# Two-block model kernel: rotary tiles taken from the projection's PSUM bank, swaps placed inside the projections, values projected last

## What is computed (reference, cut)

```python
def apply_rope(x, cos, sin):                      # first block, heads of 64
    xs = x.reshape(x.shape[:-1] + (2, 2, HEAD_DIM // 4))
    rot = jnp.stack([-xs[..., 1, :], xs[..., 0, :]], axis=-2).reshape(x.shape)
    return x * cos[None, :, None, :] + rot * sin[None, :, None, :]

for layer in range(2):                            # first block
    h_x, h_c = modulate(rmsnorm(x, ...), ...), modulate(rmsnorm(ctx, ...), ...)
    mixer = mixer_ab if layer == 0 else mixer_c   # differential + neighbourhood; grouped, banded, sinks
    x = x + gate * mixer(h_x, h_c)
    x = x + gate * swiglu(modulate(rmsnorm(x, ...), ...), w1, w3, w2)
    ...                                           # the same for ctx in layer 0

# mixer_c: q 1024, k 256, v 256 columns of h @ w_in; apply_rope on q_x and k_x, not on the context's
# swa_sink_attention (a0, a3): q 1024, k 256, v 256 columns of x @ w_qkv
    q = apply_rope_2(q, cos, sin); k = apply_rope_2(k, cos, sin)
    scores = where(valid, q @ k.T * HD ** -0.5, NEG)
    probs = softmax(concat([scores, sink]))[..., :-1]
    return (probs @ v) @ w_o
# mla_attention (m2): c = x @ w_down; cq, ckv, k_rope = split(c, [384, 640])
    q_nope, q_rope = split(rms_norm(cq) @ w_uq); k_nope, v = split(rms_norm(ckv) @ w_ukv)
    q_rope, k_rope = apply_rope_2(q_rope), apply_rope_2(k_rope)

for l in range(4):                                # second block
    x = layer_norm(ALPHA * x + mixer_l(x))
    x = layer_norm(ALPHA * x + memory_cross_attention(x))
    x = layer_norm(ALPHA * x + conv_glu_ffn(x))
```

## Time and profile before

| what | value |
|---|---|
| median of 3 runs | 2978.76 us (2978.33 to 2980.78) |
| the profiled execution's own time | 2978.18 us |
| its span in the trace | 2976.2 us |
| TensorE busy | 2682.5 us, 90% |
| TensorE weight loads (overlap) | 2507.1 us, 84% |
| POOL busy | 1872.4 us, 63% |
| ScalarE busy | 1472.4 us, 49% |
| VectorE busy | 1110.4 us, 37% |
| mean granted clock of TensorE | 0.951 |
| read from HBM | 418.52 MB, 141 GB/s over the span |

### The profile page before, as it was taken

The page is one execution under the profiler, slowest core; times in us unless marked ns, Lnnn a source line. Parts: engine busy times, 40 slices in busy tenths (PEclk is TensorE's granted clock), DMA queues, the critical chain, the costliest instruction groups (busy, mean ns, idle before and its releaser), DMA issues.

```text
span 2976.2 us, 54012 instructions
## 1 busy us (share of the span) xinstructions
PE 2682.5 (90%) x19652; PEld 2507.1 (84%) x19652; DVE 1110.4 (37%) x2614; ACT 1472.4 (49%) x2572; POOL 1872.4 (63%) x789
## 2 busy tenths in 40 slices
PE   5999898999988989998889987899888899888997
PEld 2887778999976789997889987799868899777997
DVE  3126634111144521225343365433343433463334
ACT  4316644434444544445555565555545555454555
POOL 6436646878845778872468855388635588525686
PEclk8998999999999999999999998999999999989999
DMA  6224434545533545541345533255323355313453
GB/s 242 88 75 144 147 113 132 186 162 177 184 112 128 184 148 179 186 148 66 109 135 184 182 121 115 91 178 182 134 85 114 110 181 184 133 58 114 143 182 127
DMA packets 115043, 421.45 MB, mean 142 GB/s; under 512 B 12768, under 2 KB 13792, under 8 KB 114400
## 3 DMA queue, kind: packets, MB, share of 16 engines
q1 hardware_dynamic: 114336, 413.39, 41.9%
q10 hardware_dynamic: 576, 6.23, 0.5%
HBM read 418.52 MB, written 1.05 MB: 141 GB/s over the span
## 4 chain that ended last, share of the span: by engine, by line
issue 46%; POOL 28%; PE 23%; DVE 2%; ACT 1%; POOLq 1%; ACTq 0%; DVEq 0%
POOL ring_low L1972 28%; PE bank L545 7%; PE bank L546 7%; PE bank L547 7%; ACT ring_high L1036 0%; POOLq L1975 0%; DVE rstd L1461 0%; DVE scr L1440 0%; PE bank L661 0%; PE bank L658 0%; POOLq L1971 0%; DVE scr L1516 0%; ACT xt L1113 0%; ACT high L1115 0%; DVE xt L1539 0%
## 5 line engine op out<-in xcount | busy, mean ns | idle before, releaser
L1972 POOL TENSOR_TENSOR ring_low<-ring,ring_high 128x1024 fp32r<-128x1024 f32 x785 | 1872.2, 2406 | 1082.7 <-ACT ring_high L1036 734.8
L545 PE MATMUL bank<-high,ring_high 128*128 128x256 f32 (+1 forms) x4052 | 1200.6, 296 | 156.9 <-DVE low L1523 59.9
L546 PE MATMUL bank<-low,ring_high 128*128 128x256 f32 (+1 forms) x4052 | 1191.4, 294 | 0.0
L547 PE MATMUL bank<-high,ring_low 128*128 128x256 f32 (+1 forms) x4052 | 1190.4, 294 | 0.0
L545 PEld LDWEIGHTS bank<-high,ring_high 128*128 128x128 f32 x4052 | 800.4, 198 | 180.5 <-DVE low L1523 63.4
L546 PEld LDWEIGHTS bank<-low,ring_high 128*128 128x128 f32 x4052 | 800.2, 197 | 8.6
L547 PEld LDWEIGHTS bank<-high,ring_low 128*128 128x128 f32 x4052 | 799.4, 197 | 8.7
L1237 ACT ACTIVATE ring_high<-ring 128x1024 fp32r<-128x1024 f32 x462 | 479.0, 1051 | 33.4 <-PE bank L545 33.3
L1036 ACT ACTIVATE ring_high<-ring 128x1024 fp32r<-128x1024 f32 x323 | 338.6, 1053 | 181.5 <-PE bank L545 87.3
L545 PE MATMUL bank<-hid_high,ring_high 128*128 128x256 f32 x1232 | 350.2, 284 | 9.7 <-DVE hid_low L1732 9.7
L546 PE MATMUL bank<-hid_low,ring_high 128*128 128x256 f32 x1232 | 349.5, 284 | 0.0
(11 more groups left out here) (195 smaller groups left out, 2842.7 us busy)
## 6 DMA issues: line engine op xcount, KB each, us to landing
ring<-in_units SPq DMA_DIRECT2D x785, 512.0 KB, 3.3
xt<-in_x ACTq DMA_DIRECT2D x1, 2048.0 KB, 14.0
nbias<-in_bias ACTq DMA_DIRECT2D x1, 1536.0 KB, 7.8
consts<-in_consts ACTq DMA_DIRECT2D x1, 1472.0 KB, 8.3
vt<-in_mem ACTq DMA_DIRECT2D x1, 1024.0 KB, 7.4
out_x<-xt SPq DMA_DIRECT2D x8, 128.0 KB, 1.7
cols<-in_cols SPq DMA_DIRECT2D x1, 711.0 KB, 8.1
```

Of the source, the lines that this page charges most:

```text
L545: first = pe.matmul(out, w[0], x[0], start=start, stop=False, **more)
L546: pe.matmul(out, w[0], x[1], start=False, stop=False, **more)
L547: return first, pe.matmul(out, w[1], x[0], start=False, stop=stop, **more)
L1972: pool.tensor_tensor(whole(ring_low, u), whole(ring, u), whole(ring_high, u).bitcast(fp32), ALU.subtract).then_inc(unit_ready, 1)
```

## The change

Four things, all by hand in the engines' programs. (1) **Formula.** VectorE no longer reads an evacuated tile. `spin` waits for the projection's bank and makes two products of it: bank x (-scale) x sin into a scratch slot (`turned`), bank x scale x cos into the tile itself. TensorE swaps the scratch slot instead of the tile, and `rope` is one addition of bank 4 or 5 and the tile. ScalarE evacuates none of these tiles; in `ab` and for the keys of `c` it still copies the context's half (`context_half`), and the spin there waits for it. (2) **Place of the swaps.** The swap of tile m is issued behind tile m + 1 of the same projection (the keys' two behind the first query tile; in `ab` behind tile m + 3; in `m2` behind the next query tile, the last behind the first key tile, and that of the down projection's tile 5 behind the first norm's statistics). (3) **Order.** In `c`, `a0` and `a3` the projection order, and the order of the weight units, is keys, queries, values instead of keys, values, queries; the last query tile's swap stands behind the values. (4) **Feeds.** Where ScalarE no longer evacuates it runs the feeds alone (`feed_each`); in `a0` and `a3` one more `feed`, `late=UNITS[st] + 11`, stands in the second item of the attention, and in `c` two feeds of the twelve now stand with the values. `release` is also called on the matmuls of the attention's probabilities x values, all but the last of an item.

In `ab` VectorE does four spins, then four additions, twice, ahead of the values' copies. In `m2` the squares of the first norm are no longer queued on ScalarE behind the evacuation of tile 5, and the spin of that tile stands ahead of the first norm on VectorE, its addition behind the second norm.

```diff
+        def turned(slot):
+            return scr[:, 4096 + T * (slot % 4):4096 + T * (slot % 4) + T]
...
-                def rotate(st, m, src):
+                def rotate(st, m, slot=0):
                     b = 4 + m % 2
                     claim(b)
                     pe.wait_ge(*when(st, "out", m))
-                    pe.matmul(banks[b][:, 0:T], const("swap", P), src, start=True, stop=True
+                    pe.matmul(banks[b][:, 0:T], const("swap", P), turned(slot + m), start=True, stop=True
                               ).then_inc(*mark(rot_ready, st, "rot", m))
-                    reader[b] = (st, "rotread", m)
+                    reader[b] = (st, "rope", m)
...
+                                if at < len(blocks) - 1:
+                                    release(mm)
...
-                project("ab", UNITS["ab"], 16, split(0, 2 * T), 2 * T, ready=lambda k: ("n01", "h", k))
+                def turn_ab(m):
+                    if m - 3 in ROT0:
+                        rotate("ab", m - 3)
+
+                project("ab", UNITS["ab"], 16, split(0, 2 * T), 2 * T, ready=lambda k: ("n01", "h", k), after=turn_ab)
                 project_v("ab", UNITS["ab"] + 16, 4, tokens(0, 2 * T), 4)
-                for m in ROT0:
-                    rotate("ab", m, (Q2 if m < 8 else K2)(m % 8)[:, 0:T])
...
+                def turn_behind(q, k):
+                    def after(m):
+                        if m == 0:
+                            rotate(k, 0, 2)
+                            rotate(k, 1, 2)
+                        else:
+                            rotate(q, m - 1)
+                    return after
...
                         project(st + "k", u, 2, split(0), T, ready=xready)
-                        for m in range(2):
-                            rotate(st + "k", m, K1(m))
-                        project_v(st + "v", u + 2, 1, tokens(0), 2)
-                        project(st + "q", u + 4, 8, split(0), T)
-                        for m in range(8):
-                            rotate(st + "q", m, Q1(m))
+                        project(st + "q", u + 2, 8, split(0), T, after=turn_behind(st + "q", st + "k"))
+                        project_v(st + "v", u + 10, 1, tokens(0), 2)
+                        rotate(st + "q", 7)
...
-                        rotate(st + "d", 5, K1(8))
                         stats(st + "cq", None, tiles=3)
+                        rotate(st + "d", 5)
                         stats(st + "ckv", None, tiles=2)
                         project(st + "uq", UNITS[st + "_uq"], 12, split(0), T, depth=3, per_unit=2,
-                                ready=lambda k: (st + "cq", "h", k))
-                        for m in range(4):
-                            rotate(st + "uq", 8 + m, Q1(8 + m))
+                                ready=lambda k: (st + "cq", "h", k),
+                                after=lambda m: rotate(st + "uq", m - 1) if m > 8 else None)
                         up = lambda k: split(0)(4 + k)
                         project(st + "uk", UNITS[st + "_ukv"], 8, up, T, depth=2, per_unit=4,
-                                ready=lambda k: (st + "ckv", "h", k))
+                                ready=lambda k: (st + "ckv", "h", k),
+                                after=lambda m: rotate(st + "uq", 11) if m == 0 else None)
...
+                def context_half(st, tiles, dst, u0, scale=1.0):
+                    for m in tiles:
+                        feed(u0 + m)
+                        act.wait_ge(*when(st, "proj", m))
+                        act.activation(dst(m)[:, T:2 * T], banks[m % 4][:, T:2 * T], ACT.Copy, scale=scale
+                                       ).then_inc(*mark(act_done, st, "half", m))
+
+                def feed_each(u0, n):
+                    for m in range(n):
+                        feed(u0 + m)
...
+                        if s == 1 and late is not None:
+                            feed(late)
...
-                        evacuate(st + "k", 2, K1, UNITS[st])
-                        evacuate(st + "q", 8, Q1, UNITS[st] + 4, scale=lambda m: -HD ** -0.5)
-                        attention(st + "t", gqa_items(256, swa_masks, True, COLS["sinks_a"] + 16 * (l // 3)))
+                        feed_each(UNITS[st], 10)
+                        attention(st + "t", gqa_items(256, swa_masks, True, COLS["sinks_a"] + 16 * (l // 3)),
+                                  late=UNITS[st] + 11)
...
-                        evacuate(st + "d", 6, lambda m: K1(8) if m == 5 else spare(m), UNITS[st + "_down"])
+                        evacuate(st + "d", range(5), spare, UNITS[st + "_down"])
+                        feed(UNITS[st + "_down"] + 5)
...
-                def rope(st, m, x, kind):
-                    b = 4 + m % 2
+                def spin(st, m, x, kind, scale=1.0, slot=0, halved=False):
+                    dve.wait_ge(*when(st, "proj", m))
+                    if halved:
+                        dve.wait_ge(*when(st, "half", m))
+                    b = banks[m % 4][:, 0:T]
+                    dve.scalar_tensor_tensor(out=turned(slot + m), in0=b, scalar=-scale, in1=const("sin" + kind, T),
+                                             op0=ALU.mult, op1=ALU.mult)
+                    dve.scalar_tensor_tensor(out=x, in0=b, scalar=scale, in1=const("cos" + kind, T),
+                                             op0=ALU.mult, op1=ALU.mult).then_inc(*mark(dve_done, st, "out", m))
+
+                def rope(st, m, x):
                     dve.wait_ge(*when(st, "rot", m))
-                    s = scr[:, 4096 + T * (m % 4):4096 + T * (m % 4) + T]
-                    dve.tensor_tensor(s, banks[b][:, 0:T], const("sin" + kind, T), ALU.mult
-                                      ).then_inc(*mark(dve_done, st, "rotread", m))
-                    link(dve.tensor_tensor(x, x, const("cos" + kind, T), ALU.mult))
-                    dve.tensor_tensor(x, x, s, ALU.add).then_inc(*mark(dve_done, st, "rope", m))
+                    dve.tensor_tensor(x, banks[4 + m % 2][:, 0:T], x, ALU.add).then_inc(*mark(dve_done, st, "rope", m))
+
+                def spin_queries(q, k, keys, kind):
+                    for m in range(8):
+                        spin(q, m, Q1(m), kind, scale=-HD ** -0.5)
+                        if m == 0:
+                            rope(k, 0, keys(0))
+                            rope(k, 1, keys(1))
+                        else:
+                            rope(q, m - 1, Q1(m - 1))
```

75 lines of the change are left out of this document (41 added, 34 removed).

## The result

| | us |
|---|---|
| before, 4 runs | 2978.55 median (2978.03 to 2980.78) |
| changed kernel, 4 runs | 2947.36 median (2942.52 to 2954.82) |
| ratio | 0.9896, 95% interval 0.9873 to 0.9919 |
| the changed kernel's profiled execution | 2954.82, the slowest of the four; span 2953.0, clock 0.955 |

The change gains 31 us, 1.0%; 39 were forecast. 2947.4 lies inside the range (2927 to 2953), but outside the forecast's own case (2930 to 2945). The runs of the changed kernel spread over 12 us where those of before spread over 3, and that spread turns out to be part of the explanation.

What follows compares the result with a forecast made beforehand. TensorE was taken as the bound, busy 90% of the span, so only its standing time could be saved. Gaps -29.6, clock -14.5, late feeds +4.2 and c's feed +0.7 gave -39.2 us, hence 2939 us, range 2927 to 2953.

Steps and rivals of the forecast that it cites:

- the forecast's own case: Whole kernel: the predicted main outcome, 2930 to 2945 us around 2939, with chance 0.53.
- The gap and its prices: Projections to first scores, and m2's norm: moved swaps cost about 0.53 us each, old gaps shrink; -29.6 us in all.
- tail of 1.52 us: Last swap's start to first scores: 0.63 to VectorE's start, 0.42 addition, 0.47 to scores; 1.0 beyond the swap's 0.53.
- Rival 5: Projections: swaps inside stall TensorE for the previous tile's spin, only m2's norm gain of 2.6 remains; 2976 us, chance 0.02.
- Rival 3: m2: only half its gain comes, projections being bound by POOL and the ring; +4.6, 2943.6 us, chance 0.07.
- Rival 4: Query tiles: spins held up by POOL, 5.4 us against TensorE's 3.41, 24 tiles late 2.0 each; 2987 us, chance 0.03.
- The clock term: Attention starts regain full clock: ab 3.0, c 3.5, a0 3.0, a3 3.0, plus m2's key tiles 2.0; -14.5 us.
- rival 1: Attention starts: a tail of 1 us still lowers the clock, only m2's -2 of -14.5 stays; 2951.5 us, chance 0.20.
- (b): c's attention: the values' last two units are owed into it and its first feed waits; +0.7 us.
- (c): Attention: `release` only adds a semaphore to matmuls already there; 0, +-1 us.
- The late feed: a0 and a3, attention item two: two copies of 1.05 us delay evacuations; 2.1 us per layer, +4.2 in all.
- rival 2: a0's and a3's attention: late feeds' POOL passes slow VectorE's L1615, 2.2 us more per layer; 2943.4 us, chance 0.10.

Runs made afterwards that it cites:

- r5_place: Kernel before with only the query swaps moved, each behind the next tile of its projection in ab, c, a0, a3; values first, old formula: 2959.02 us, 0.9922.
- r2_filled: Kernel before with each query swap of ab, c, a0 and a3 issued twice, filling part of TensorE's idle: 2971.98 us, 0.9964.
- r6_order: Changed kernel with values projected ahead of queries again in c, a0, a3, and no late feed: 2934.81 us, 0.9849; repeated, 2935.97 us, 0.9848.
- r9_fill: Changed kernel with filling swaps behind the first scores, four in c, two each in a0 and a3: 2943.12 us, 0.9871.
- r11_bestfill: Changed kernel with values before queries, no late feed, values' copy awaited at probabilities x values, four filling swaps behind c's first scores: 2936.74 us, 0.9859.
- r7_tail: Changed kernel with last query swap mid values' projection and values' copy awaited only at first probabilities x values, five rotary mixers: 2941.79 us, 0.9874.
- r1_again: The changed kernel run again, unaltered, for its spread and a second profile: 2945.53 us median, 0.987.
- r4_late6: Changed kernel with the late feed of a0's and a3's attention moved from the second item to the seventh: 2947.73 us, 0.989.

## Why the prediction was right, and where not

- **The gap and its prices: right.** Swap between tiles, tail of 1.52 us, spins of 0.42 us hidden behind the next tile, copies and statistics in `m2`: every stretch to the scores is within 0.8 us of its term, -33.7 against -31.6. Rival 5 (the gaps only move) is out. Rival 3 (`m2` gains half) is out: -2.7 and -6.6 against -2.6 and -6.6. That the place of the swaps is what brings most of this is shown by r5_place (21 us); what the formula, `m2`'s changes and the keys' swaps add has no run to itself.
- **Rival 4, the slower case: out, and its price was wrong.** Spins are never held up. And the price of two long steps per tile came from single rows; r5_place shows mostly one per tile, so that even the old formula fits inside the projection. The 466 ns given as L1416's median was that of eleven key tiles; over the 32 query tiles it was 415. No run evacuates first and then uses the new formula; the steps on evacuated tiles take 408 ns at their fastest and up to 2589 in r5_place, those on a bank 414 to 426.
- **The clock term failed in part.** I wrote that the swaps' gap is "the only thing before these stretches that is not before `m2`'s attention" and took 12.5 us for four attentions. r2_filled shows what filling half of the idle is worth by itself: 10 us. In `ab` it came back (-3.9 against -3.0), though the same `ab` code gives 219.9 to 224.0 us in other profiles, -1.8 to -5.9. r6_order shows the term's size in `a3` (3.3 against 3.0). In `a0`, and in `a3` in one of two profiles, the changed kernel loses the level 4 to 7 us behind the first scores. This is the outcome of rival 1 in one or two places of four, but not its mechanism: values first has 0.5 us more idle in front and keeps the level in all eight attentions. `m2`'s attention, my proof against the rival, itself falls to 0.5 in three of the profiled executions.
- **`c`: the clock came back, and the time was lost again.** r2_filled has the same first 13 us in `c` as the changed kernel (48 matmuls, 0.87) and gains 2.9 of the 3.5 us there; the changed kernel gains 0.1. TensorE's waits in `c`'s attention, r2_filled, then the changed kernel:

```profile
PE bank L791 <- DVE scr L1607: 2.4, 7, 0.3
...
PE bank L624 <- ACT ada_cols L1074: 0.3, 1, 0.3
```

```profile
PE bank L795 <- DVE scr L1653: 4.2, 6, 0.8
...
PE bank L628 <- ACT ada_cols L1096: 1.9, 1, 1.9
```

These are the same two places, and 3.4 us more idle; there is also one more short fall of the level, 97.5 us behind the first scores. So beside the clock 2.8 us were lost in `c`'s attention, where the sum had (b) +0.7 and (c) 0 for feeds and `release`. The new idle is there with values first too (r6_order) and not in r5_place; which of the formula, the feeds and the `release` calls makes it, no run shows. The fall behind `c`'s first scores comes from the idle of 2.56 us there: with it filled the level holds, twice (r9_fill, r11_bestfill), for 1 to 2 us.
- **The late feed was undersized.** It was put at 2.1 us per layer. Where the level stays at 1.00 until the feed (`a3` in the first profile and in r9_fill, `a0` in r7_tail), the stretch is 63.2, 63.2 and 63.3 us against 59.7 with values first: 3.5 us. Of this 2.03 us is the idle that I had costed; VectorE beside POOL (2.13 us at L1663, rival 2) and 3.4 us at half clock behind the idle are the rest. I had these as separate cases; here they come together. The remaining loss, up to 2.3 us per layer, is not the feed's: in r1_again (5.8 and 5.2 us longer) the level is down from 4.1 and 6.9 us behind the scores, and the feed comes at 14.9 and 14.4. There, with TensorE at half clock, it makes no idle of its own; L795's waits for ScalarE in `a3` are those of r6_order, which has no late feed:

```profile
PE bank L795 <- ACT scr L1170: 1.2, 2, 1.0
```

- **The sum.** 39.2 forecast, 31.2 measured, 33 with all eight runs (2978.55 - 2945.6). Without `m2`'s fall the profile's attentions give 9.6 - 10.8 = -1.2 against -7.6, so 6.4 us of the forecast are missing there (3.5 in `a0`, 2.7 in `c`, 1.1 in `a3`, less 0.9 that `ab` gave more); the stretches to the scores give 2.1 more than forecast, and 0.9 is lost elsewhere: 39.2 - 6.4 + 2.1 - 0.9 = 34.0. The number came out inside the range by its width, which rival 1 had stretched. `m2`'s fall was in no term and in no rival, and the two runs that lie near 2955 us, both profiled with it, are above the range.

Open: why the level falls in `a0` in both profiles of the changed kernel and in `a3` only in the second, when TensorE's idles around the first scores are the same in `a0` and `a3` of the first (0.93, 1.19 and 0.47 us); why it falls in none of the eight `a0` and `a3` attentions of the four profiles with values first and the new formula, where the idle in front is no shorter; and what decides `m2`'s attention between 57.3 and 68.1 us.

## What to carry to other kernels

When a serial chain of small steps stands between a projection and its consumer, put its matrix step inside the projection, one tile behind: the place alone gave 21 us. Let the elementwise steps read the PSUM bank: with it the tail was as long as worked out from single rows. Before moving a stage to the end as cover, ask what its buffers were handing back: here values last hid 0.6 to 2.0 us three times, held two weight units into the attention, and cost 3.5 to 5.8 us twice. A copy put into a stage where two engines are near balance costs its own time, what its follow-up work does to a third engine, and the clock behind the idle: 3.5 us where 2.1 were costed.

## What the runs showed of the hardware

- TensorE's granted level stood at 0.5 for 24 us of unbroken work (24.00 busy of 24.00, 65 matmuls) in one execution (r1_again) and at 1.00 in that of another kernel with the same code in this stage (r4_late6: 23.31 busy, 122 matmuls). A busy TensorE is not a fast one, and the two differ by 10.8 us, a third of this change's gain.
- Adding 32 swaps that compute what is already there, in idle time, made the kernel before 10 us faster (ratio 0.9964, 0.995 to 0.9977).
- A VectorE step with both operands in SBUF goes from 0.42 to a median of 2.27 us when it stands beside POOL's passes regularly (32 instances in r5_place), one with a bank as operand stays at 414 to 426 ns in 107 instances. The Trainium skill's "SBUF — State Buffer", section "Who interferes with whom", says that the first kind contends with GpSimd and the second does not, and the trace agrees.
